# Half products joined, norm pairs, and one modulation group moved from TensorE to VectorE in a two-block float32 transformer kernel

## The chip, the cores and the metric

The program runs on one core of a Trainium2 chip. The metric is the device time of one execution in microseconds (us). The kernel before takes 2903.88 us (median of 3 runs, 2903.18 to 2905.7).

## What is computed

Four residual layers over 256 latent tokens and 256 context tokens of width 2048, float32 throughout. In every layer both streams are normalised and modulated, projected in, mixed, projected out and added back through a gate:

```python
shift, scale, gate = jnp.split(silu(c) @ mod_w[i] + mod_b[i], 3)      # one row for latent, one for context
h  = rms_norm(x,   norm_g[i]) * (1 + scale)  + shift
hc = rms_norm(ctx, norm_g[i]) * (1 + cscale) + cshift
y, yc = mixer(h @ w_in, hc @ w_in) @ w_out
x, ctx = x + gate * y, ctx + cgate * yc        # the context only where it is needed later
```

Layer 0 mixes with a gated linear recurrence (RG-LRU), layer 1 with differential attention over 16 heads. Layers 2 and 3 join a spatial gating unit (SGU, 8 groups) with grouped-query attention (8 heads); they have a context of their own (ctx_2) and condition vectors of their own. Layers 1 and 3 need no context output, so their out projections have 256 columns; those of layers 0 and 2 have 512.

## The kernel before

**Strips.** Every projection weight is cut into strips: 16 tiles of 128x128, 1 MB, one output tile of 128 rows each; there are 248. Strips stream through four half slots `raw` (two strips, `load_strip` on SyncE's queue). A float32 product is made from split halves: ScalarE rounds the weights to `w_hi` (`split_hi`, L221), VectorE takes the rest, `w_lo = raw - w_hi` (`split_lo`, L229), the activations lie as `h_hi` and `h_lo`, and TensorE runs three products per weight tile (`strip`, L247 to L249): high by high, high by low, low by high. `w_hi` and `w_lo` hold two strips, so the weights of strip s+2 are made while strip s+1 runs, and only after strip s is done. Each engine has its own written order of instructions (`lru_pe`, `lru_dve`, ...) and the engines meet in semaphores.

**Modulation.** The 4 x 3 x 2048 modulation values for two condition rows are products of a condition vector with 201 MB of weights, worked in beside the strips in two ways. A *group* (`mod_load`, `mod_chunk`, `mod_rows`, `mod_turn`, `mod_add`) gives 512 values: 4 chunks of 1 MB, 4 products each on TensorE (L261), a copy on ScalarE, a turn by small products (L284). A *unit* (`unit_load`, `unit`) gives 128 values on VectorE: two halves of 512 KB, and per half two multiply-and-accumulate passes over 1024 elements (L334 for the latent row, L336 for the context row), then one small add (L339). Units need the condition rows as silu(c) in `cb` (`cb_load` on GpSimd's queue, `cb_tanh` on ScalarE, `cb_silu` on VectorE, L304, L311, L318). `UNIT_PLAN` says how many whole units stand behind each tile of the out projections of layers 0 and 2. A half's slot is loaded again once VectorE has used it. Layer 3's scale is made by 4 groups (`SGU_MODS`, `M_SGU`) in layer 2's first four SGU groups; layer 3's shift by units in layer 2's out projection, its gate by units in layer 3's SGU.

**Out projection** (`out_first`, `out_pe`, `out_act`, `out_dve`, `out_pool`): 16 tiles in two PSUM banks. After tile m VectorE adds it to the residual (L651, L653) and splits strip m+2; in layers 0 and 2 its units follow. ScalarE splits, then squares the new tile (L557, L558), GpSimd adds the squares (L600) and scales x for the next norm (L602), and issues the units' loads (L326). In layer 1 the squares wait for the load of ctx_2.

**Norm** (`norm_pe`, `norm_sqrt`, `norm_act`, `norm_dve`): small products (L401) sum the squares, 1/sqrt comes back as rows (L406, L416), and then VectorE and ScalarE make h tile by tile (L453, L454, L436, L461). The first strip of the next layer takes each k tile of h as it becomes ready (`operand=` of `strip`); the second strip comes after it.

## Time and profile before

| | before |
|---|---|
| median of 3 runs | 2903.88 us |
| the profiled execution | 2906.17 us |
| its span, first to last instruction | 2904.5 us |
| TensorE (PE) busy | 2716.9 us, 94% |
| PE weight loads (PEld) busy | 2184.1 us, 75% |
| VectorE (DVE) busy | 1847.6 us, 64% |
| ScalarE (ACT) busy | 1213.4 us, 42% |
| GpSimd (POOL) busy | 314.1 us, 11% |
| mean granted TensorE clock | 0.969 of full |
| moved | 488.89 MB, 168 GB/s |

The profile is one execution; times in it are counted from its first instruction. Busy is the union of an engine's own instructions; matmuls are pipelined and overlap in the records, so the pace of TensorE is read from the distance of their starts, not from their durations. A bracket behind a row of the timeline is the idle time of that engine before the row and what ended it. The layers' stretches are: layer 0 with the start 0 to 745 us (its out projection from 570), layer 1 to 1615 (out projection from 1527), layer 2 to 2430 (SGU 1620 to 1950, out projection from 2257), layer 3 to the end.

### The profile page before, as it was taken

The page shows a single profiled execution, that of the slowest core. Times are in us where ns is not written, and L with a number is a line of the kernel's source. Part 1 is how long each engine was busy: PE and PEld are TensorE (multiplying, and loading weights), DVE is VectorE, ACT ScalarE, POOL GpSimd, SP SyncE. Part 2 cuts the span into 40 slices and gives each one's busy share as a digit, 9 for nine tenths or more (in the row PEclk, how much of TensorE's full clock was granted, in tenths as well). Part 3 has the DMA queues.
Part 4 walks back from the last instruction along what each step waited for, and adds up shares of the span by engine and source line. Part 5 has one row for each costly group of instructions (what it writes and reads, how often), then busy time and mean ns, then how long its engine had stood idle before and what let it go on. Part 6 is the DMA issues. An engine that isn't in the chain of part 4 may idle for free.

```text
span 2904.5 us, 41776 instructions
## 1 busy us (share of the span) xinstructions
PE 2716.9 (94%) x14482; PEld 2184.1 (75%) x14482; DVE 1847.6 (64%) x2772; ACT 1213.4 (42%) x1859; POOL 314.1 (11%) x437
## 2 busy tenths in 40 slices
PE   5799999889899999999989899999998998999989
PEld 1477777668677777777779677888886776998879
DVE  4399999889656565565665522334545887775654
ACT  3355655512434434443444422323444314553643
POOL 1111001044000000000004100000000442110000
PEclk7899999999999999999999999999999997999999
DMA  9755445367455554455535454322221664883325
GB/s 377 276 173 180 153 158 184 127 212 231 143 190 187 181 196 167 180 182 187 179 116 188 157 181 149 98 95 87 73 72 44 214 206 128 278 281 114 127 93 168
DMA packets 118631, 488.89 MB, mean 168 GB/s; under 512 B 13584, under 2 KB 15632, under 8 KB 103440
## 3 DMA queue, kind: packets, MB, share of 16 engines
q1 hardware_dynamic: 74176, 267.49, 27.3%
q0 software_dynamic: 44368, 220.22, 22.4%
q8 instruction: 56, 0.92, 0.1%
q14 instruction: 31, 0.25, 0.0%
HBM read 485.56 MB, written 2.10 MB: 168 GB/s over the span
## 4 chain that ended last, share of the span: by engine, by line
PE 67%; DVE 17%; issue 7%; DMA 5%; ACT 2%; DVEq 1%; POOL 0%; ACTq 0%; POOLq 0%; SPq 0%
PE psum L247 17%; PE psum L249 17%; PE psum L248 17%; DVE psum L334 4%; DVE w_lo L229 4%; PE psum L261 3%; DMA work<-in_mod_units 2%; DVE work L336 2%; DMA y<-in_mod_weights 2%; PE psum L974 1%; PE psum L1457 1%; PE psum L937 1%; DVE work L820 1%; ACT w_hi L221 1%; PE psum L284 1%
## 5 line engine op out<-in xcount | busy, mean ns | idle before, releaser
L247 PE MATMUL psum<-h_hi,w_hi 128*128 128x512 f32 (+1 forms) x3808 | 1359.8, 357 | 59.6 <-DVE h_lo L461 33.8
L249 PE MATMUL psum<-h_hi,w_lo 128*128 128x512 f32 (+1 forms) x3808 | 1323.6, 348 | 0.0
L248 PE MATMUL psum<-h_lo,w_hi 128*128 128x512 f32 (+1 forms) x3808 | 1323.0, 347 | 0.0
L229 DVE TENSOR_TENSOR w_lo<-raw,w_hi 128x1024 fp32r<-128x1024 f32 x496 | 597.5, 1246 | 587.9 <-ACT w_hi L221 587.8
L247 PEld LDWEIGHTS psum<-h_hi,w_hi 128*128 128x128 f32 x3808 | 728.6, 191 | 180.5 <-DVE w_lo L229 38.3
L248 PEld LDWEIGHTS psum<-h_lo,w_hi 128*128 128x128 f32 x3808 | 729.6, 192 | 93.7 <-issue 10.0
L249 PEld LDWEIGHTS psum<-h_hi,w_lo 128*128 128x128 f32 x3808 | 728.7, 191 | 88.7
L221 ACT ACTIVATE w_hi<-raw 128x1024 fp32r<-128x1024 f32 x496 | 496.7, 1052 | 283.0 <-PE psum L249 269.5
L334 DVE SCALAR_TENSOR_TENSOR psum<-work,modraw 128x1024 f32<-128x1024 f32 x128 | 177.7, 1389 | 24.3 <-DMA work<-in_mod_units 24.0
L336 DVE SCALAR_TENSOR_TENSOR work<-work,modraw 128x1024 f32<-128x1024 f32 x128 | 162.2, 1267 | 0.0
L267 POOL DMA_DIRECT2D modraw<-in_mod_weights x80 | 42.4, 530 | 822.6 <-PE psum L261 813.4
L261 PE MATMUL psum<-modraw,cond 128*32 128x512 f32 x768 | 110.8, 655 | 12.1 <-DMA modraw<-in_mod_weights 8.8
L326 POOL DMA_DIRECT2D work<-in_mod_units x128 | 68.1, 532 | 490.4 <-DVE work L336 473.1
L557 ACT ACTIVATE work<-xl 128x256 f32 (+1 forms) x48 | 19.8, 413 | 198.5 <-DVE xl L653 191.0
L600 POOL TENSOR_TENSOR work<-work 128x512 f32<-128x512 f32 x39 | 74.4, 1909 | 81.7 <-ACT work L558 81.7
L1001 ACT ACTIVATE y<-psum 128x512 f32<-128x512 f32 x16 | 9.6, 597 | 169.6 <-PE psum L249 169.6
L531 PE MATMUL psum<-h_hi,w_hi 128*128 128x256 f32 (+1 forms) x128 | 49.5, 386 | 30.0 <-DVE h_lo L516 30.0
L726 PE MATMUL psum<-work 128*128 128x512 f32 x128 | 59.2, 605 | 19.1 <-DVE work L820 19.1
L1027 ACT ACTIVATE y<-psum 128x512 f32<-128x512 f32 x16 | 9.6, 597 | 146.1 <-PE psum L249 146.1
L653 DVE SCALAR_TENSOR_TENSOR xl<-psum,mod,xl 128x256 f32 (+1 forms) x48 | 23.1, 481 | 67.3 <-PE psum L249 66.0
L1082 DVE RECIPROCAL work<-work 128x256 f32<-128x256 f32 x16 | 28.0, 1753 | 50.0 <-ACT work L1014 50.0
L726 PEld LDWEIGHTS psum<-work 128*128 128x128 f32 x128 | 23.0, 190 | 48.6 <-issue 40.2
(260 smaller groups left out, 2705.0 us busy)
## 6 DMA issues: line engine op xcount, KB each, us to landing
raw<-in_weights SPq DMA_DIRECT2D x496, 512.0 KB, 4.5
modraw<-in_mod_weights POOLq DMA_DIRECT2D x96, 1024.0 KB, 5.3
work<-in_mod_units POOLq DMA_DIRECT2D x128, 512.0 KB, 4.5
y<-in_mod_weights POOLq DMA_DIRECT2D x16, 1024.0 KB, 8.9
modraw<-in_mod_units POOLq DMA_DIRECT2D x32, 512.0 KB, 4.6
modraw<-in_cond_rows POOLq DMA_DIRECT2D x4, 1024.0 KB, 6.4
work<-in_gate_w POOLq DMA_DIRECT2D x16, 256.0 KB, 5.0
work<-in_x_t POOLq DMA_DIRECT2D x16, 256.0 KB, 3.6
```

The costliest lines, as they stand in the source:

```text
L221: act.activation(w_hi[:, par, half, :], raw[:, 2 * par + half, :], ACT.Copy).then_inc(S["split_hi"], 1)
L229: dve.tensor_tensor(w_lo[:, par, half, :], raw[:, 2 * par + half, :], w_hi[:, par, half, :].bitcast(F32), ALU.subtract).then_inc(S["split_ ...
L247: pe.matmul(dst, hi, h_hi[:, k, 0:n], start=(k == 0), stop=False)
L248: pe.matmul(dst, hi, h_lo[:, k, 0:n], start=False, stop=False)
L249: mm = pe.matmul(dst, lo, h_hi[:, k, 0:n], start=False, stop=(k == KT - 1))
L261: mm = pe.matmul(bank[32 * j:32 * j + 32, :], cond[:, 4 * q + j, :], chunk[:, j, :], start=(q == 0), stop=(q == 3))
L326: pool.dma_start(mw[:, half, :], ins["mod_units"][2 * p + half]).then_inc(unit_in[half], 16)
L334: dve.scalar_tensor_tensor(out=junk, in0=mw_work[:, half, :], scalar=0.5, in1=cb[:, 0, part], op0=ALU.mult, op1=ALU.mult, accum_out=macc[: ...
L336: dve.scalar_tensor_tensor(out=mw_work[:, half, :], in0=mw_work[:, half, :], scalar=0.5, in1=cb[:, 1, part], op0=ALU.mult, op1=ALU.mult, a ...
L531: pe.matmul(psum[:, c, 0:n], hi, h_hi[:, k, 0:n], start=(k == 0), stop=False)
L600: pool.tensor_tensor(acc, acc, sqb[c], ALU.add).then_inc(S["sq_added"], 1)
L726: pe.matmul(psum[:, GATE_BANK + g, :], lw["gw"][par][:, g, :], lw["xc"], start=True, stop=True).then_inc(L["gate_done"], 1)
```

## The change

1. **Layers 1 and 3, out projection.** `h_hi` and `h_lo` become two halves of one tensor `h_both`. `both` multiplies a high weight tile with 256 columns of h's high part and 256 of its low part in one product of 512 columns, which leaves two half results in a bank; the low weights add 256 columns. VectorE adds both half results to x, one after the other, with a semaphore between.
2. **Norm pair.** The first two strips of layers 1, 2 and 3 run together, k tile by k tile (`first_pair`), as layer 0's did. Two of the three sums of squares run in and behind the last strip of the out projection (`norm_sums`). The split of the second strip's second half stands behind the first four tiles of h.
3. **Layer 3's scale** comes from 16 units in layer 2's SGU, four halves per SGU group (`light`), loaded into the free upper half of y; the 4 TensorE groups are gone. The second network's condition rows are therefore prepared twice: in the first two tiles of layer 1's out projection, and in layer 2's as before.
4. **Halves.** The plan of layers 0's and 2's out projections counts half units behind each tile (`HALVES`), at most 3, and their tiles are written out instead of looped.

```diff
-        h_hi = sb("h_hi", [P, KT, NT], F32R)
-        h_lo = sb("h_lo", [P, KT, NT], F32R)
+        h_both = sb("h_both", [P, 2, KT, NT], F32R)
+        h_hi, h_lo = h_both[:, 0, :, :], h_both[:, 1, :, :]
...
+        def both(pe, bank, k, hi, lo):
+            joined = bank.rearrange("p (a t) -> p a t", a=2)
+            if k < KT - 1:
+                pe.matmul(joined, hi, h_both[:, :, k, 0:T], start=(k == 0), stop=False)
+                return pe.matmul(bank[:, 0:T], lo, h_hi[:, k, 0:T], start=False, stop=False)
+            pe.matmul(bank[:, 0:T], lo, h_hi[:, k, 0:T], start=False, stop=False)
+            return pe.matmul(joined, hi, h_both[:, :, k, 0:T], start=False, stop=True)
...
+        def first_pair(pe, s, dsts, ready, k0, k1):
+            for k in range(k0, k1):
+                half, kk = divmod(k, HALF)
+                pe.wait_ge(S["h_ready"], ready + k + 1)
+                for c, (dst, n) in enumerate(dsts):
+                    if kk == 0:
+                        pe.wait_ge(S["split_lo"], 2 * (s + c) + half + 1)
+                    hi, lo = (w[:, c, half, kk * P:(kk + 1) * P] for w in (w_hi, w_lo))
+                    pe.matmul(dst, hi, h_hi[:, k, 0:n], start=(k == 0), stop=False)
+                    pe.matmul(dst, hi, h_lo[:, k, 0:n], start=False, stop=False)
+                    mm = pe.matmul(dst, lo, h_hi[:, k, 0:n], start=False, stop=(k == KT - 1))
+                    if k == KT - 1:
+                        mm.then_inc(S["strip_done"], 1)
...
+        mw_y = y[:, 0, HALF:, :].rearrange("p (h k) t -> p h (k t)", h=2)
...
+        CB_NET = [0, 1, 1]
+        CB_IN = [1, 2 + 2 * (MOD_GROUPS - MOD_FIRST), 3 + 2 * (MOD_GROUPS - MOD_FIRST)]
...
+            if half == 1:
+                dve.wait_ge(S["unit_used"], 2 * p + 2)
+                dve.scalar_tensor_tensor(out=mod[:, bass.ds(slot, 1), :], in0=macc[:, par:par + 1, :, 0], scalar=col("mod_b", slot),
+                                         in1=macc[:, par:par + 1, :, 1], op0=ALU.add, op1=ALU.add).then_inc(S["unit_cols"], 1)
+                dve.wait_ge(S["unit_cols"], p + 1)
...
-        UNIT_PLAN = {0: [(0, 1, 2, 2), (1, 4, 1, 1), (4, 5, 2, 1), (5, 6, 1, 1), (6, 7, 1, 1), (7, 8, 0, 0)],
-                     1: [(0, 1, 0, 0), (1, 7, 0, 0), (7, 8, 0, 0)],
-                     2: [(0, 1, 0, 0), (1, 2, 2, 2), (2, 4, 1, 1), (4, 5, 2, 2), (5, 6, 1, 1), (6, 7, 1, 1), (7, 8, 0, 0)],
-                     3: [(0, 7, 0, 0), (7, 8, 0, 0)]}
...
+        HALVES = {0: (U_OUT0 - 1, [2, 1, 2, 2, 3, 2, 3, 2, 3, 3, 3, 2, 3, 3, 0, 0]),
+                  2: (U_OUT2, [0, 0, 2, 3, 3, 2, 3, 3, 2, 3, 3, 2, 3, 3, 0, 0])}
+        def halves_of(l, m):
+            if l not in HALVES:
+                return []
+            p, counts = HALVES[l]
+            n = sum(counts[:m])
+            return [(p + (n + i) // 2, (n + i) % 2) for i in range(counts[m])]
...
+        def norm_sums(pe, l, parts):
+            for n in parts:
+                sq = (acc, sqb[0], sqb[1])[n]
+                if n == 0:
+                    pe.wait_ge(S["sq_added"], added_base[l + 1])
+                    ge(pe, S["unit_used"], 2 * UNITS_READY[l])
+                else:
                     pe.wait_ge(S["sq_done"], KT * (l + 1) - 2 + n)
                 for t in range(NT // P):
                     mm = pe.matmul(psum[:, SS_BANK, t:t + 1], sq[:, t * P:(t + 1) * P], ones[:, 0:1],
                                    start=(n == 0 and t == 0), stop=(n == 2 and t == NT // P - 1))
-            mm.then_inc(S["ss_done"], 1)
+            if n == 2:
+                mm.then_inc(S["ss_done"], 1)
+        def norm_pe(pe, l):
+            norm_sums(pe, l, (2,) if l > 0 else (0, 1, 2))
...
+            high(0)
+            split_hi(act, layer_strip[l] // 2, 1, halves=(1,))
+            with act.Fori(1, KT // 4) as j:
+                high(j)
...
+            four(0)
+            split_lo(dve, layer_strip[l] // 2, 1, halves=(1,))
+            with dve.Fori(1, KT // 4 - 1) as j:
+                four(j)
...
+                    if wide[l]:
+                        pe.matmul(psum[:, c, 0:n], hi, h_hi[:, k, 0:n], start=(k == 0), stop=False)
+                        pe.matmul(psum[:, c, 0:n], hi, h_lo[:, k, 0:n], start=False, stop=False)
+                        mm = pe.matmul(psum[:, c, 0:n], lo, h_hi[:, k, 0:n], start=False, stop=(k == KT - 1))
+                    else:
+                        mm = both(pe, psum[:, c, :], k, hi, lo)
...
+            one(KT // 2 - 1, 0)
+            one(KT // 2 - 1, 1, (lambda half: norm_sums(pe, l + 1, ((0,), (1,))[half])) if l < 3 else None)
...
+                if l == 1:
+                    if c == 0:
+                        act.wait_ge(S["mod_cols"], MOD_GROUPS)
+                    cb_tanh(act, 1, (2 * c, 2 * c + 1))
...
+                        for p, half in halves_of(l, 2 * j + c):
+                            if p + 1 not in (U_SGU2, U_SGU):
+                                unit_load_half(pool, p + 1, half, mw_work)
...
+                else:
+                    dve.scalar_tensor_tensor(out=xl[:, m, :], in0=psum[:, c, T:NT], scalar=gate(0),
+                                             in1=xl[:, m, :], op0=ALU.mult, op1=ALU.add).then_inc(S["x_half"], 1)
+                    dve.wait_ge(S["x_half"], KT * (l // 2) + m + 1)
...
+                if isinstance(j, int) and j == 0 and l == 1:
+                    cb_silu(dve, 1, (2 * c, 2 * c + 1))
...
+            pool.wait_ge(S["mod_used"], 4 * MOD_GROUPS)
+            cb_load(pool, 1)
...
+                    first_pair(pe, S_ATT, [(psum[:, K_BANK, :], NT), (psum[:, Q_BANK, 0:T], T)], KT, 0, KT)
+                    for q in range(2):
+                        chunk(q)(1)
...
+            unit_load(pool, first, mw)
+            with pool.Fori(0, GROUPS // 2 - 1) as j:
+                for par in range(2):
+                    units(2 * j + par)
+                    table(2 * j + 2 + par, par, False)
+            units(GROUPS - 2)
+            unit_load(pool, first + KT - 1, mw)
...
+                    first_pair(pe, layer_strip[2 + lay], [(psum[:, GU_BANK, 0:n], n), (psum[:, GV_BANK, 0:n], n)], KT * (2 + lay), 0, KT)
...
-                    if mods:
-                        mod_chunk(pe, M_SGU + i, 3)
-                        mod_turn(pe, M_SGU + i, 1)
...
+                if lay == 0:
+                    unit_half(dve, U_SGU2 + 2 * i + n // 2, n % 2, n // 2, 9 * KT + SCALE + 2 * i + n // 2, mw_y)
```

Three places show how the order moves.

VectorE in layer 2's SGU, the second group from the split that follows its second strip on (`work` holds most buffers, `modraw` the condition rows, `y` in the change the unit's weights), before:

```order
L229 TENSOR_TENSOR w_lo<-raw,w_hi 128x1024 x2
L1303 SCALAR_TENSOR_TENSOR work<-work,psum 128x512
L229 TENSOR_TENSOR w_lo<-raw,w_hi 128x1024 x2
L1308 TENSOR_REDUCE small<-work 128x4
L291 TENSOR_TENSOR mod<-psum,cols 128x8
L1312 RECIPROCAL small<-small 128x4
L1316 TENSOR_SCALAR work<-psum,small 128x128 x4
```

With the change:

```order
L228 TENSOR_TENSOR w_lo<-raw,w_hi 128x1024 x2
L376 SCALAR_TENSOR_TENSOR psum,small<-y,modraw 128x1024
L378 SCALAR_TENSOR_TENSOR y,small<-y,modraw 128x1024
L382 SCALAR_TENSOR_TENSOR mod<-small,cols 128x2
L1360 SCALAR_TENSOR_TENSOR work<-work,psum 128x512
L228 TENSOR_TENSOR w_lo<-raw,w_hi 128x1024 x2
L376 SCALAR_TENSOR_TENSOR psum,small<-y,modraw 128x1024
L378 SCALAR_TENSOR_TENSOR y,small<-y,modraw 128x1024
L1365 TENSOR_REDUCE small<-work 128x4
L1367 RECIPROCAL small<-small 128x4
L1371 TENSOR_SCALAR work<-psum,small 128x128 x4
L376 SCALAR_TENSOR_TENSOR psum,small<-y,modraw 128x1024
```

A half unit (L376 and L378, every second one with the add L382) now stands behind each split and another behind the scaled tiles; the add for the TensorE group, L291, is gone.

ScalarE at the start of layer 1's out projection, from the last high copy of y on, before:

```order
L511 ACTIVATE h_hi<-y 128x256
L221 ACTIVATE w_hi<-raw 128x1024 x2
L557 ACTIVATE work<-xl 128x256
L558 ACTIVATE work<-y 128x256
L221 ACTIVATE w_hi<-raw 128x1024 x2
L557 ACTIVATE work<-xl 128x256
L558 ACTIVATE work<-y 128x256
```

With the change:

```order
L572 ACTIVATE h_both<-y 128x256
L220 ACTIVATE w_hi<-raw 128x1024 x2
L629 ACTIVATE work<-xl 128x256
L630 ACTIVATE work<-y 128x256
L350 ACT_TABLE_LOAD
L350 ACTIVATE work<-modraw 128x1024 x2
L220 ACTIVATE w_hi<-raw 128x1024 x2
L629 ACTIVATE work<-xl 128x256
L630 ACTIVATE work<-y 128x256
L350 ACTIVATE work<-modraw 128x1024 x2
```

The tanh of the condition rows stands between the first tile's squares and the next strip's split, with a table load ahead of it.

TensorE at the start of layer 2, before, where the next rows go on with the first strip alone:

```order
L401 MATMUL psum<-consts,work 128x1 x12
L406 MATMUL psum<-consts,small 128x128 x4
L247 MATMUL psum<-h_hi,w_hi 128x512
L248 MATMUL psum<-h_lo,w_hi 128x512
L249 MATMUL psum<-h_hi,w_lo 128x512
L247 MATMUL psum<-h_hi,w_hi 128x512
L248 MATMUL psum<-h_lo,w_hi 128x512
L249 MATMUL psum<-h_hi,w_lo 128x512
```

With the change (each weight tile pair of the first strip is followed by the second strip's, to the end of both):

```order
L451 MATMUL psum<-consts,work 128x1 x8
L460 MATMUL psum<-consts,small 128x128 x4
L285 MATMUL psum<-h_both,w_hi 128x512
L286 MATMUL psum<-h_both,w_hi 128x512
L287 MATMUL psum<-h_both,w_lo 128x512
L285 MATMUL psum<-h_both,w_hi 128x512
L286 MATMUL psum<-h_both,w_hi 128x512
L287 MATMUL psum<-h_both,w_lo 128x512
L285 MATMUL psum<-h_both,w_hi 128x512
L286 MATMUL psum<-h_both,w_hi 128x512
```

The two strips' products alternate by k tile, and four of the twelve sums of squares (L401, now L451) have left this place for the middle of the last strip; the next four stand directly behind that strip.

## Rows read from the trace of the kernel before

**Rows 1.** The page, part 4: the chain that ended last, by engine.

```profile
PE 67%; DVE 17%; issue 7%; DMA 5%; ACT 2%; DVEq 1%; POOL 0%; ACTq 0%; POOLq 0%; SPq 0%
```

**Rows 2.** Waits of TensorE: us in total, times, longest.

```profile
PE psum L247 <- DVE h_lo L461: 33.8, 42, 4.5
```

**Rows 3.** Timeline of TensorE (start us, us), two 512-column and two 256-column products.

```profile
742.75 0.39 PE L247 MATMUL psum<-h_hi,w_hi 128*128 128x512 f32 x1
742.98 0.39 PE L248 MATMUL psum<-h_lo,w_hi 128*128 128x512 f32 x1
...
1560.01 0.28 PE L249 MATMUL psum<-h_hi,w_lo 128*128 128x256 f32 x1
1560.13 0.28 PE L247 MATMUL psum<-h_hi,w_hi 128*128 128x256 f32 x1
```

**Rows 4.** Timeline of VectorE, layer 2's SGU: groups 1 and 2, then 4 and 5.

```profile
1715.83 0.69 DVE L1303 SCALAR_TENSOR_TENSOR work<-work,psum 128x512 f32<-128x512 f32 x1 [8.80 <-ACT work L1253]
...
1756.56 0.69 DVE L1303 SCALAR_TENSOR_TENSOR work<-work,psum 128x512 f32<-128x512 f32 x1 [8.80 <-ACT work L1253]
...
1835.63 0.69 DVE L1303 SCALAR_TENSOR_TENSOR work<-work,psum 128x512 f32<-128x512 f32 x1 [7.57 <-ACT work L1253]
...
1869.68 0.69 DVE L1303 SCALAR_TENSOR_TENSOR work<-work,psum 128x512 f32<-128x512 f32 x1 [7.49 <-ACT work L1253]
...
1893.83 2.36 DVE L229 TENSOR_TENSOR w_lo<-raw,w_hi 128x1024 fp32r<-128x1024 f32 x2 [5.78 <-ACT w_hi L221]
```

**Rows 5.** Timeline of ScalarE and VectorE, first strips of layers 2 and 3.

```profile
1650.24 0.60 ACT L1243 ACTIVATE work<-psum 128x512 f32<-128x512 f32 x1 [0.67 <-PE psum L249]
1662.35 0.60 ACT L1248 ACTIVATE work<-psum 128x512 f32<-128x512 f32 x1 [9.63 <-PE psum L249]
...
2462.47 0.39 ACT L1243 ACTIVATE work<-psum 128x256 f32<-128x256 f32 x1 [0.71 <-PE psum L249]
2463.84 2.36 DVE L229 TENSOR_TENSOR w_lo<-raw,w_hi 128x1024 fp32r<-128x1024 f32 x2 [2.46 <-ACT w_hi L221]
2470.12 0.39 ACT L1248 ACTIVATE work<-psum 128x256 f32<-128x256 f32 x1 [5.38 <-PE psum L249]
```

**Rows 6.** Windows: us, busy us (instructions) by engine, granted clock, DMA share, GB/s.

```profile
2432.50:2466.60 34.10, 21.93 (x77) 17.28 (x77) 29.42 (x69) 19.96 (x39) 2.17 (x4) 0.50 0.22 62
```

**Rows 7.** TensorE's groups by line, out projections of layers 0 and 2.

```profile
L247 PE MATMUL psum<-h_hi,w_hi 128*128 128x512 f32 x224 | 89.1, 398 | 12.3 <-DVE w_lo L229 12.3
...
L247 PE MATMUL psum<-h_hi,w_hi 128*128 128x512 f32 x222 | 88.7, 399 | 9.6 <-DVE w_lo L229 9.6
```

**Rows 8.** Timeline of VectorE and GpSimd, layer 0's out projection: units.

```profile
584.87 1.23 DVE L334 SCALAR_TENSOR_TENSOR psum<-work,modraw 128x1024 f32<-128x1024 f32 x1 [5.83 <-DMA work<-in_mod_units]
587.16 1.23 DVE L334 SCALAR_TENSOR_TENSOR psum<-work,modraw 128x1024 f32<-128x1024 f32 x1
...
597.06 0.53 POOL L326 DMA_DIRECT2D work<-in_mod_units  x1 [1.99 <-DVE work L336]
...
601.75 1.23 DVE L334 SCALAR_TENSOR_TENSOR psum<-work,modraw 128x1024 f32<-128x1024 f32 x1 [2.44 <-DMA work<-in_mod_units]
...
696.34 0.48 DVE L651 SCALAR_TENSOR_TENSOR y<-psum,mod,work 128x256 f32<-128x256 f32 x1
...
705.88 0.48 DVE L651 SCALAR_TENSOR_TENSOR y<-psum,mod,work 128x256 f32<-128x256 f32 x1
```

**Rows 9.** Timeline, layer 1's out projection, and ScalarE's tanh (ns min/median/max).

```profile
1536.99 0.42 ACT L557 ACTIVATE work<-xl 128x256 f32<-128x256 f32 x1 [7.46 <-DMA y<-in_ctx_t]
...
1540.17 0.39 PE L247 MATMUL psum<-h_hi,w_hi 128*128 128x256 f32 x1 [3.37 <-DVE w_lo L229]
...
L311 ACT ACTIVATE work<-modraw x8: 1041/1054/1062, 131.1 to 2268.6; 128x1024 f32<-128x1024 f32 x8
L311 ACT ACT_TABLE_LOAD  x1: 1283/1283/1283, 129.4 to 129.4; - x1
```

**Rows 10.** Timeline of TensorE, sums of squares before layer 1.

```profile
743.43 2.94 PE L401 MATMUL psum<-consts,work 128*128 128x1 f32 x24
```

272 lines of the change are left out of this document (115 added, 157 removed).

## The prediction

> **What bounds the kernel now.** I read first the chain that ended last: 67% of it is TensorE, 17% VectorE [rows 1]. The second view is TensorE's own waits, because an idle microsecond there is worth a microsecond: the longest sum, 33.8 us, is its wait for h, in the norms [rows 2], and in the out projections of layers 0 and 2 it waits 12.3 and 9.6 us for low weights [rows 7]. The third is TensorE's pace where it waits for nothing: 227 ns from one 512-column product to the next, 120 ns at 256 columns [rows 3], so a strip is 48 x 0.227 = 10.9 us or 48 x 0.120 = 5.76 us. The kernel is bound by TensorE's issue nearly everywhere; what counts is work taken off TensorE, and waits of TensorE that go or come.
>
> **Layer 3's scale leaves TensorE.** In layer 2's SGU a group with modulation takes 1756.56 - 1715.83 = 40.73 us, one without 1869.68 - 1835.63 = 34.05 us [rows 4]: 6.7 us a group, 4 groups, -26.7 us; I take -26.5. In return VectorE gets 32 half units. A half is 587.16 - 584.87 = 2.3 us [rows 8], with the small add 9.7 us per group of 34. They are free if they fit where VectorE idles: in the groups without modulation it waits 5.8 us before a split [rows 4], and 7.5 us before L1303. A half of 2.3 us fits ahead of each. The loads come four to a 34 us group, far apart against the 601.75 - 597.06 = 4.7 us from issue to landing [rows 8]; GpSimd's queue holds only tables between them. Without that cover a half costs its 2.3 us.
>
> **Norm pair.** VectorE's and ScalarE's pace of h is untouched, so the last k tile is ready as late as before; what goes is the second strip behind it. But no weights of a third strip can be made before both of the pair are done, and that is a new wait. In layer 3 the first strip's result is read at 2462.47 and VectorE begins the next split at 2463.84; half a split later (1.2 us), 2.6 us after the read began and 3.0 after the strip, TensorE can go on [rows 5]. Layer 2: second strip now 10.9 us behind the first; then one more k tile (3 x 0.227 = 0.7) and the 3.0 wait: -7.2 us. Layer 3: now 2470.12 - 2462.47 = 7.65 us [rows 5], as TensorE ran at half its clock (1.2 GHz) until 2466.6 after a norm in which it had little to do [rows 6]; then 0.4 + 3.0: -4.3. Layer 1: the second strip has 256 columns, 5.8 us; two modulation chunks stand behind the pair and cover 2 of the 3.5 us: -5. Sum 16.5; I take -16, since the pair is denser work for a slowed clock but the new wait may bring another slow stretch. Nothing is late next: the following strips find their splits early. Bounds: -20 (no new wait) and -9 (the wait and a slow stretch behind each).
>
> **Sums of squares.** 24 small products take 2.9 us, 0.11 each, mostly while ScalarE squares the last tile [rows 10]. Eight of them go into the last strip, where they are on the path: 0.9 us, three times, less what the end gains; VectorE is late there in two of the three. +1.2 us (0 to 2.7).
>
> **Joined halves.** Per weight tile three 256-column products, 3 x 0.120 = 0.360, become 0.227 + 0.120 = 0.347 [rows 3]: 13 ns, over 2 x 16 x 16 tiles 6.7 us. The rows give 13 ns of fixed time per product over N/2.4. By the Trainium skill (TensorE: Matmul & The Clock Gate, Back-to-back issue gap) the isolated distance of two matmuls is N/2.4 + 2.5 ns, which speaks against this edit: one product less would be worth 2.5 ns, 1.3 us in all. The trace decides for 13 ns. VectorE's second add, 0.48 us as L651's [rows 8], hides behind ScalarE's split, except after each layer's last tile: +0.9. Net -5.8 (0 if one 512-column product costs as much as two of 256).
>
> **Condition rows in layer 1.** ScalarE squares the first tile at 1536.99, when ctx_2 has landed, and TensorE's fourth strip waits until 1540.17 [rows 9]. Now a table load (1.28) and two tanh (2 x 1.05) stand between those squares and the fourth strip's split: squares done 1537.7, tanh 1541.1, first half high 1542.1. VectorE, after two silu passes of about 1.2 and two adds, splits from 1543.7: TensorE starts at 1544.9, +4.7. The second pair of tanh and silu does the same with less: +1.2. After 8 us of idling some half clock follows: +2. Sum +7.9 (3 to 11). The second load of the condition rows, 2 MB, goes out behind the last group's weights long before ctx_2's, and costs nothing.
>
> **Halves.** In layer 0 a tile with a whole unit takes 705.88 - 696.34 = 9.54 us on VectorE [rows 8], of a strip of 10.9: 4.6 us for the tile (with what GpSimd's adds hold up) and 2.3 a half, 0.24 for the add. Double units overran, behind tiles 0, 1 and 8. The new plan spreads the same halves; its tiles with 3 still have one wait: the third half's load is issued when the first is used, lands 4.7 later, and the second half covers 2.4, so 2.3 us of waiting and 14.1 us a tile. I walked both plans tile by tile: tile m starts on VectorE at the later of strip m's end and its own end of tile m-1; low weights for strip m+2 are there 4.2 us after; TensorE starts strip m+2 at the later of that and the end of strip m+1. The old plan so walked stands 10.4 us in layer 0 and 8.5 in layer 2 (traced: 12.3 and 9.6 [rows 7]), the new one 6.8 and 9.4, mostly in tiles 11 to 15, where 3, 3 and 3 follow each other. With the slow stretches after the old stalls, and one tile evacuated late: -6 in layer 0, -1.3 in layer 2. With landings in 4.0 us it stalls 2.9 and 4.8; with 5.5, 11.9 and 15.3.
>
> **Sum.** -26.5 - 16 + 1.2 - 5.8 + 7.9 - 6 - 1.3 = -46.5 us. The profiled execution took 2906.2, so 2859.7; the median run lies 2.3 lower, 2857.4. Forecast **2857 us**.
>
> **Rivals.**
> - *Third halves land late.* The out projections load 1.5 MB of units beside 1 MB of weights per tile. For: VectorE already waited 2.4 and 5.8 us there [rows 8]. Against: those loads ran beside the same weights. At 5.5 us landing 5 + 6 us more stalls, and 2 of half clock: 2870. Chance 0.20.
> - *Landings are quick and the new waits short.* At 4.0 us the walk loses 8.5 us of stalls, with 4 of half clock: 2845. Chance 0.17.
> - *The join does nothing*: the change does not do what it says if the two half streams are walked apart and a 512-column product costs 240 ns. 2864. Against: every 512-column product takes 227 ns. Chance 0.05.
> - *Slower: half units ahead of the splits in layer 2's SGU.* VectorE's order is fixed, so a half that comes late holds the split behind it, and TensorE a strip later. If each of the 32 held TensorE for its full 2.3 us and the adds 4: +78, 2857 + 78 = 2935. It decides once VectorE's idle time ahead of a split is under 2.3 us; the rows have 5.8. Chance 0.02.
>
> **The numbers.** Main case 0.56 (2850 to 2865). The range takes in the first two rivals and the bounds of pair and condition rows: 2843 to 2874; about 1 in 10 lies outside on each side at most. A measurement can tell about 0.2%, 6 us: faster 0.97, within it 0.01, slower 0.02.
>
> **What would show it.** Layer 2's SGU: all groups at 34 us, no wait of TensorE for low weights. Norms: no idle time per k tile worth a second strip, but one wait of about 3 us behind each pair in layers 2 and 3, 1 to 2 in layer 1. Layer 1's out projection: a wait of 8 us ahead of the fourth strip, then starts of weight tiles 0.347 apart. Layers 0 and 2: VectorE waiting some 2.3 us for a load in each tile with three halves, TensorE for low weights near the end. It is wrong if a 34 us group grows, if the pair's end moves against h's last tile, or if the stalls in layers 0 and 2 go altogether.

## The result and the profile after

The changed kernel takes 2875.94 us in the median of four runs (2873.26 to 2877.19), the kernel before, beside it, 2904.3: a ratio of 0.9902, 95% interval 0.9888 to 0.9916. That is 28.4 us gained, where 46.5 were forecast, and 2 us above the upper end of the range.

| | after |
|---|---|
| the profiled execution | 2876.43 us |
| its span | 2874.7 us |
| TensorE (PE) busy | 2694.6 us, 94% |
| VectorE (DVE) busy | 1942.7 us, 68% |
| mean granted TensorE clock | 0.967 of full |

The page of after, part 4, the chain that ended last: TensorE holds 65% of it, 2 points less than in [rows 1], and VectorE 20%, 3 points more.

```profile
PE 65%; DVE 20%; issue 7%; DMA 6%; ACT 2%; DVEq 1%; POOL 0%; ACTq 0%; POOLq 0%; SPq 0%
```

The waits of TensorE over the whole span (us in total, times, longest), beside [rows 2] and [rows 7]:

```profile
PE psum L285 <- DVE h_both L518: 16.6, 23, 3.7
PE psum L246 <- DVE w_lo L228: 15.6, 7, 3.2
PE psum L451 <- DVE work L378: 10.9, 2, 6.1
PE psum L259 <- DVE w_lo L228: 8.6, 3, 8.0
```

L285 is `first_pair`, L246 `strip`, L259 the joined product, L451 the sums of squares. The wait for h fell from 33.8 us to 16.6, as the pair should make it. The third row is new: 10.9 us, in two waits, in which TensorE stands ahead of the sums of squares until VectorE's last half unit is through.

**Where the time went.** I cut both spans at the same places, by the end of a strip's last product in TensorE's timeline, and do so for every kernel run below (one profiled execution each, us). "Out+norm" is an out projection with the norm behind it, up to the end of the fourth strip of the next layer. A column called a stage below is one of these:

| | up to layer 0's out | layer 0 out+norm | attention | layer 1 out | norm, layer 2 up to its out | layer 2 out+norm | layer 3 up to its out | layer 3 out |
|---|---|---|---|---|---|---|---|---|
| before | 537.9 | 266.4 | 690.1 | 122.3 | 588.9 | 276.2 | 301.2 | 118.4 |
| after | 536.8 | 264.4 | 690.2 | 125.8 | 555.9 | 278.7 | 302.8 | 116.5 |
| sums_behind | 535.8 | 264.2 | 691.8 | 126.4 | 555.4 | 278.4 | 304.1 | 116.8 |
| sums_own_bank | 533.2 | 262.0 | 690.2 | 126.7 | 555.6 | 275.3 | 304.0 | 115.1 |
| before_sums_moved | 533.6 | 265.6 | 690.1 | 122.6 | 592.1 | 282.5 | 301.2 | 116.8 |
| out_halves_short | 538.9 | 243.6 | 691.8 | 125.6 | 556.7 | 260.4 | 301.4 | 114.9 |
| whole_units | 535.3 | 252.8 | 690.2 | 126.1 | 555.5 | 265.9 | 303.8 | 115.0 |
| before_units_spread | 533.2 | 260.4 | 691.8 | 120.2 | 587.9 | 272.2 | 301.0 | 118.4 |
| pair_apart | 540.4 | 271.7 | 691.8 | 125.8 | 563.0 | 281.2 | 304.1 | 116.6 |
| join_apart | 537.8 | 266.2 | 691.7 | 127.7 | 555.3 | 278.0 | 301.0 | 116.8 |
| join_adjacent | 539.4 | 264.0 | 690.1 | 125.3 | 556.7 | 279.1 | 302.5 | 116.7 |
| rows_spread | 535.2 | 265.4 | 690.1 | 122.3 | 556.8 | 280.7 | 301.0 | 116.6 |
| sgu_halves_short | 539.1 | 267.0 | 690.1 | 125.6 | 555.6 | 278.3 | 301.0 | 115.1 |
| best | 539.9 | 254.3 | 690.2 | 121.8 | 555.3 | 269.9 | 305.8 | 116.8 |

Two things are scatter from one execution to the next. The first column moves by 7 us between kernels whose code is the same there. And stretches at half clock (a granted clock of 0.50, 1.2 GHz) come and go elsewhere: one of 3.4 us makes the 1.6 us more of after in the column of layer 3 up to its out; in layer 2's attention after has 13.6 us of them and before 6.8, and the 3.5 us more that it takes stand in the column of layer 2's out+norm. Differences of 3 us and less in one column mean little.

Read so, the change did in its stages: layer 0's out projection with its norm -2.0 (forecast -10.6: halves -6, pair -5, sums +0.4), layer 2's +2.5 (forecast -5.2), the norm and SGU of layer 2 -33.0 (forecast -33.3), layer 1's out projection +3.5 (forecast +5.0). The two stages that hold half units are short of the forecast by 16 us, 3.5 of them the scatter in layer 2's attention, and nothing else is off by more than 2.

Each of the two stages has two parts, the out projection up to the end of its last strip and the norm behind it. The norms are 4.7 and 4.9 us shorter than before (56.0 against 60.8, 48.0 against 52.9). Layer 0's out projection is 2.7 us longer (208.35 against 205.66), layer 2's 4.0 longer from the end of its second strip on (171.7 against 167.7). So it is the out projections that miss the forecast.

In layer 2's SGU every group takes what a group without modulation took, 1837.08 - 1803.02 = 34.06 us, early ones too (1734.88 - 1700.90 = 33.98), where [rows 4] had 40.73 for an early one. Timeline of VectorE, after (start us, us, ..., idle before it and who ended that):

```profile
1700.90 0.69 DVE L1360 SCALAR_TENSOR_TENSOR work<-work,psum 128x512 f32<-128x512 f32 x1 [5.10 <-ACT work L1311]
...
1734.88 0.69 DVE L1360 SCALAR_TENSOR_TENSOR work<-work,psum 128x512 f32<-128x512 f32 x1 [4.79 <-ACT work L1311]
...
1803.02 0.69 DVE L1360 SCALAR_TENSOR_TENSOR work<-work,psum 128x512 f32<-128x512 f32 x1 [4.80 <-ACT work L1311]
...
1837.08 0.69 DVE L1360 SCALAR_TENSOR_TENSOR work<-work,psum 128x512 f32<-128x512 f32 x1 [4.70 <-ACT work L1311]
```

The end of layer 0's out projection, timeline of VectorE, after. A third half (L376) waits for its load, 2.48 us in tile 12, 2.13 in tile 13; tile 13's is through at 735.5 us, tile 14 is taken (L727) at 735.79 only, 14 us after its strip ended (721.7). In the kernel before it was taken 1.8 us after (734.5 and 732.7):

```profile
719.06 1.24 DVE L376 SCALAR_TENSOR_TENSOR psum<-work,modraw 128x1024 f32<-128x1024 f32 x1 [2.48 <-DMA work<-in_mod_units]
...
721.36 0.48 DVE L727 SCALAR_TENSOR_TENSOR y<-psum,mod,work 128x256 f32<-128x256 f32 x1
...
733.12 1.23 DVE L376 SCALAR_TENSOR_TENSOR psum<-work,modraw 128x1024 f32<-128x1024 f32 x1 [2.13 <-DMA work<-in_mod_units]
734.27 1.22 DVE L378 SCALAR_TENSOR_TENSOR work<-work,modraw 128x1024 f32<-128x1024 f32 x1
...
735.79 0.48 DVE L727 SCALAR_TENSOR_TENSOR y<-psum,mod,work 128x256 f32<-128x256 f32 x1
...
738.40 2.36 DVE L228 TENSOR_TENSOR w_lo<-raw,w_hi 128x1024 fp32r<-128x1024 f32 x2 [1.74 <-ACT w_hi L220]
745.18 0.48 DVE L727 SCALAR_TENSOR_TENSOR y<-psum,mod,work 128x256 f32<-128x256 f32 x1 [4.42 <-PE psum L248]
```

And TensorE there: in the middle of the last strip the sums of squares wait 4.82 us, and behind the wait the products come 0.43 us apart (737.91, 738.34), where they come 0.227 apart at full clock:

```profile
730.44 0.39 PE L248 MATMUL psum<-h_both,w_lo 128*128 128x512 f32 x1
735.64 1.84 PE L451 MATMUL psum<-consts,work 128*128 128x1 f32 x8 [4.82 <-DVE work L378]
737.91 0.63 PE L247 MATMUL psum<-h_both,w_hi 128*128 128x512 f32 x1
738.34 0.63 PE L248 MATMUL psum<-h_both,w_lo 128*128 128x512 f32 x1
```

The granted clock (the column behind the five engines' busy times) is at its lower level, 1.2 GHz, for 6.8 us there and for 10.2 us at the like wait in layer 2's last strip, which ends at 2394.0. The first 0.6 and 3.6 us of them still lie in the waits. Behind them TensorE loses 3.0 and 3.2 us, by the starts of its products (those up to the first at full pace took 6.62 and 7.52 us, and would take 3.6 and 4.3 at the distances seen at full clock, 0.227 and for the sums 0.112):

```profile
735.00:741.80 6.80, 6.16 (x19) 5.22 (x20) 3.96 (x7) 2.62 (x4) 0.61 (x1) 0.50 0.12 41
2390.40:2400.60 10.20, 6.55 (x20) 5.52 (x21) 5.84 (x9) 2.62 (x4) 0.61 (x1) 0.50 0.13 48
```

### The profile page after: what moved, and what is told of

It is laid out like the page before. It is cut to its first block, busy times and chain, and to the rows that moved or that the text cites. A ratio compares the mean times of both kernels' runs of the same rounds, so it can differ in the third digit from the quotient of the medians.

```text
span 2874.7 us, 40435 instructions
## 1 busy us (share of the span) xinstructions
PE 2694.6 (94%) x13810; PEld 2159.6 (75%) x13810; DVE 1942.7 (68%) x2948; ACT 1217.1 (42%) x1861; POOL 314.5 (11%) x455
## 4 chain that ended last, share of the span: by engine, by line
PE 65%; DVE 20%; issue 7%; DMA 6%; ACT 2%; DVEq 1%; POOL 0%; ACTq 0%; POOLq 0%; SPq 0%
PE psum L246 15%; PE psum L248 15%; PE psum L247 15%; DVE w_lo L228 5%; DVE psum L376 4%; PE psum L259 4%; PE psum L296 3%; DVE work L378 2%; DMA work<-in_mod_units 2%; DMA y<-in_mod_weights 2%; PE psum L260 2%; PE psum L1509 1%; PE psum L1012 1%; PE psum L1050 1%; DVE work L890 1%
## 5 line engine op out<-in xcount | busy, mean ns | idle before, releaser
L246 PE MATMUL psum<-h_both,w_hi 128*128 128x512 f32 (+1 forms) x3264 | 1188.3, 364 | 15.7 <-DVE w_lo L228 15.6
L248 PE MATMUL psum<-h_both,w_lo 128*128 128x512 f32 (+1 forms) x3264 | 1158.6, 355 | 0.0
L247 PE MATMUL psum<-h_both,w_hi 128*128 128x512 f32 (+1 forms) x3264 | 1158.3, 355 | 0.0
L228 DVE TENSOR_TENSOR w_lo<-raw,w_hi 128x1024 fp32r<-128x1024 f32 x496 | 607.2, 1265 | 480.2 <-ACT w_hi L220 479.3
L246 PEld LDWEIGHTS psum<-h_both,w_hi 128*128 128x128 f32 x3264 | 620.9, 190 | 112.9 <-issue 15.4
L247 PEld LDWEIGHTS psum<-h_both,w_hi 128*128 128x128 f32 x3264 | 621.1, 190 | 93.5 <-issue 9.8
L248 PEld LDWEIGHTS psum<-h_both,w_lo 128*128 128x128 f32 x3264 | 620.3, 190 | 87.0
L376 DVE SCALAR_TENSOR_TENSOR psum<-work,modraw 128x1024 f32<-128x1024 f32 x128 | 171.3, 1338 | 36.5 <-DMA work<-in_mod_units 36.0
L259 PE MATMUL psum<-h_both,w_hi 128*128 128x512 f32 x480 | 177.7, 410 | 15.6 <-DVE w_lo L228 8.6
L378 DVE SCALAR_TENSOR_TENSOR work<-work,modraw 128x1024 f32<-128x1024 f32 x128 | 158.6, 1239 | 0.0
L260 PE MATMUL psum<-h_both,w_lo 128*128 128x256 f32 x480 | 137.2, 286 | 0.0
L259 PEld LDWEIGHTS psum<-h_both,w_hi 128*128 128x128 f32 x480 | 92.9, 194 | 39.9 <-DVE w_lo L228 9.5
L296 PE MATMUL psum<-modraw,cond 128*32 128x512 f32 x640 | 93.8, 669 | 10.5 <-DMA modraw<-in_mod_weights 6.9
L260 PEld LDWEIGHTS psum<-h_both,w_lo 128*128 128x128 f32 x480 | 93.4, 195 | 1.4
L1077 ACT ACTIVATE y<-psum 128x512 f32<-128x512 f32 x16 | 9.6, 597 | 169.7 <-PE psum L248 167.7
L285 PE MATMUL psum<-h_both,w_hi 128*128 128x512 f32 (+1 forms) x128 | 54.4, 425 | 20.3 <-DVE h_both L518 16.6
L676 POOL TENSOR_TENSOR work<-work 128x512 f32<-128x512 f32 x39 | 64.4, 1651 | 75.9 <-ACT work L630 75.9
```

The costliest lines, as they stand in the source:

```text
L228: dve.tensor_tensor(w_lo[:, par, half, :], raw[:, 2 * par + half, :], w_hi[:, par, half, :].bitcast(F32), ALU.subtract).then_inc(S["split_ ...
L246: pe.matmul(dst, hi, h_hi[:, k, 0:n], start=(k == 0), stop=False)
L247: pe.matmul(dst, hi, h_lo[:, k, 0:n], start=False, stop=False)
L248: mm = pe.matmul(dst, lo, h_hi[:, k, 0:n], start=False, stop=(k == KT - 1))
L259: pe.matmul(joined, hi, h_both[:, :, k, 0:T], start=(k == 0), stop=False)
L260: return pe.matmul(bank[:, 0:T], lo, h_hi[:, k, 0:T], start=False, stop=False)
```

## The experiments

Each was timed against the kernel before on its chip, and ratios stand with their 95% intervals. A time is the median of the kernel's runs. A row of the table above is one execution only.

### Is it the new place of the sums of squares?

**sums_behind.** The first suspicion: the half units' product and the sums of squares share a PSUM bank (`junk` is banks 6 and 7, `SS_BANK` is 6), so `norm_sums` waits for all half units of the layer, and it now does so in the middle of a strip. The run puts the sums of layers 0 and 2 back behind the strip.

```
-  one(KT // 2 - 1, 1, (lambda half: norm_sums(pe, l + 1, ((0,), (1,))[half])) if l < 3 else None)
+  one(KT // 2 - 1, 1, (lambda half: norm_sums(pe, l + 1, ((0,), (1,))[half])) if l == 1 else None)
...
-  norm_sums(pe, l, (2,) if l > 0 else (0, 1, 2))
+  norm_sums(pe, l, (2,) if l == 2 else (0, 1, 2))
```

> The changed kernel with the sums of squares of layers 0 and 2 back behind the last strip. Theory A: in the last strip they wait for VectorE's last half unit, because its product goes to the same PSUM bank; that wait (4.8 and 6.1 us in the trace of the changed kernel) and the half clock behind it (8.5 us) go away: 2857 us, no wait of TensorE ahead of L451 in the middle of the last strips. Rival B: the last half units are late for the norm in any case, which waits for them itself; the wait moves behind the strip: 2872 to 2876 us.

Measured: 2875.42 us, ratio 0.9899 (0.9884 to 0.9914): no change, rival B. Layer 0's out projection is now 7.4 us shorter (200.98 against 208.35) and the norm behind it 7.2 longer (63.2 against 56.0); in layer 2 it is 10.0 and 9.6. The waits of TensorE in layer 0's stage, and VectorE at its end, in sums_behind:

```profile
PE psum L246 <- DVE w_lo L228: 9.5, 5, 3.5
PE psum L451 <- ACT work L630: 4.0, 2, 3.2
PE psum L451 <- DVE work L378: 1.3, 1, 1.3
```

```profile
735.58 1.23 DVE L376 SCALAR_TENSOR_TENSOR psum<-work,modraw 128x1024 f32<-128x1024 f32 x1 [2.49 <-DMA work<-in_mod_units]
...
738.25 0.48 DVE L727 SCALAR_TENSOR_TENSOR y<-psum,mod,work 128x256 f32<-128x256 f32 x1
...
740.86 2.36 DVE L228 TENSOR_TENSOR w_lo<-raw,w_hi 128x1024 fp32r<-128x1024 f32 x2 [1.74 <-ACT w_hi L220]
743.14 0.48 DVE L727 SCALAR_TENSOR_TENSOR y<-psum,mod,work 128x256 f32<-128x256 f32 x1
```

VectorE is done with tile 13's third half at 738.0 us, then come tile 14 and its split, and tile 15, whose strip has long ended (736.8), is taken at 743.14. Its squares (ACT L630) are what the sums then wait for. Theory A was wrong: the new place of the sums only showed where VectorE was late.

**sums_own_bank.** The sums stay in the strip, in bank 5, and the wait for the half units moves behind them. (Bank 5 is in use at the kernel's start, so the sums of the very first norm are not the kernel's.)

```
-  ge(pe, S["unit_used"], 2 * UNITS_READY[l])
...
-  mm = pe.matmul(psum[:, SS_BANK, t:t + 1], sq[:, t * P:(t + 1) * P], ones[:, 0:1],
+  mm = pe.matmul(psum[:, SUM_BANK, t:t + 1], sq[:, t * P:(t + 1) * P], ones[:, 0:1],
...
   pe.wait_ge(S["rcol_done"], l + 1)
+  ge(pe, S["unit_used"], 2 * UNITS_READY[l])
```

> The changed kernel with the sums of squares in PSUM bank 5, which nothing else uses there, in their place within the last strip, and without the wait for the half units ahead of them (it now stands ahead of the broadcast products into bank 6). Theory A (the shared bank makes the wait): 2856 us, 1 us below the version with the sums behind the strip. Rival B (the place within the strip costs by itself, since the sums also need GpSimd's last add): still a wait in the middle of the strip, 2872 us or more.

Measured: 2878.77 us (2867.45 to 2882.85), ratio 0.9911 (0.9895 to 0.9928). No gain either by the medians; its profiled execution, the fastest of the five, is 2.4 and 3.4 us shorter in the two stages, which is about what the table can tell. The expectation had not thought of what stands here: no wait in the middle of the strip, but 1.31 and 3.83 us behind it, for tile 14's and tile 15's squares.

**before_sums_moved.** The kernel before with `norm_sums` in and behind the last strip and nothing else.

```
-  pe.wait_ge(S["x_new"], KT * l + 2 * j + c - 1)
-  strip(pe, st, psum[:, c, 0:n], n)
...
+  one(KT // 2 - 1, 0)
+  one(KT // 2 - 1, 1, (lambda half: norm_sums(pe, l + 1, ((0,), (1,))[half])) if l < 3 else None)
```

> The kernel before with nothing but the sums of squares moved into and behind the last strip. Theory A: its last whole unit is done at 734.2 us, 4 us ahead of the middle of the last strip, and 2419.2 us, 4 us ahead too; so the wait for it costs nothing, and it is the new plan of halves that makes the wait: 2901 to 2904 us, no wait ahead of the sums. Rival B (the place costs by itself): 2913 to 2924 us.

Measured: 2908.48 us, ratio 1.0013 (1.0004 to 1.0022), 1 to 6 us slower. No wait ahead of the sums is in its trace; the last strips of layers 0 and 2 are 0.9 us longer each (11.8 against 10.9), and nothing comes back that the scatter would let one see (norms of 61.2 and 52.7 us against 60.8 and 52.9). So the move by itself costs what the prediction said (+1.2, 0 to 2.7) or somewhat more, and the wait comes with the plan of halves.

### Is it the plan of halves?

**out_halves_short.** Half units of one column in the out projections of layers 0 and 2. The kernel so leaves out the modulation values that they make; their loads, waits and places stay.

```
-  part = slice(half * 1024, (half + 1) * 1024)
-  dve.scalar_tensor_tensor(out=junk, in0=mw[:, half, :], scalar=0.5, in1=cb[:, 0, part], op0=ALU.mult,
+  part = slice(half * 1024, half * 1024 + n)
+  dve.scalar_tensor_tensor(out=junk[:, 0:n], in0=mw[:, half, 0:n], scalar=0.5, in1=cb[:, 0, part], op0=ALU.mult,
...
```

> The changed kernel with the half units of the out projections of layers 0 and 2 reduced to one column each (their modulation columns are left out; loads, waits and order stay). Theory C (VectorE's time in these stages is what counts): all waits of TensorE for low weights and ahead of the sums go, 18 and 19 us: 2839 us. Rival B (the loads bound it): VectorE then waits for each load, two halves a strip still fit 10.9 us, but a third waits 4.7 us: some of the waits ahead of the sums stay, 2850 to 2870 us.

Measured: 2838.52 us, ratio 0.9778 (0.9758 to 0.9797), theory C's figure. VectorE now waits 46.9 us for the loads in layer 0's stage, and TensorE waits for none of it: L246's wait for low weights is absent from its waits there, whose longest two are these.

```profile
PE psum L285 <- DVE h_both L518: 7.3, 12, 3.7
PE psum L451 <- ACT work L630: 0.9, 1, 0.9
```

```profile
L376 DVE SCALAR_TENSOR_TENSOR psum<-work,modraw 128x1 f32<-128x1 f32 x34 | 15.0, 440 | 47.5 <-DMA work<-in_mod_units 46.9
```

So the loads alone hold nobody; with the passes of the 34 halves on top of its tiles VectorE holds TensorE. That is 37 us for the 66 halves of the two stages.

**whole_units.** The same halves in another order, with the sums behind the strip. The kernel to compare it with is sums_behind, which differs in the order alone.

```
-  HALVES = {0: (U_OUT0 - 1, [2, 1, 2, 2, 3, 2, 3, 2, 3, 3, 3, 2, 3, 3, 0, 0]),
-            2: (U_OUT2, [0, 0, 2, 3, 3, 2, 3, 3, 2, 3, 3, 2, 3, 3, 0, 0])}
+  HALVES = {0: (U_OUT0 - 1, [2, 2, 2, 2, 2, 4, 2, 2, 2, 2, 4, 2, 2, 2, 2, 0]),
+            2: (U_OUT2, [0, 0, 4, 2, 2, 2, 4, 2, 2, 2, 2, 4, 2, 2, 2, 0])}
...
```

> The changed kernel with the sums of squares of layers 0 and 2 behind the last strip and the halves dealt out evenly: layer 0 [2,2,2,2,2,4,2,2,2,2,4,2,2,2,2,0], layer 2 [0,0,4,2,2,2,4,2,2,2,2,4,2,2,2,0]. Theory C: VectorE's queue bounds these two stages; the new plan pays a wait for a load (2.2 to 2.6 us) in each of its nine tiles with three halves, and what VectorE is behind at the last tile with halves the norm waits for. A tile with 2 halves waits for nothing, one with 4 waits once. Walked with the measured durations, layer 0's last strip ends at 727 us, not at 745, and VectorE is done with the last tile at 729, not 746; layer 2's 2385 and 2388, not 2404 and 2405. 2844 us, no wait of TensorE for low weights in the two stages. Rival B (what was behind is bound to the loads themselves, 512 KB each beside the weights): 2865 to 2876 us.

Measured: 2848.95 us (2847.39 to 2849.92), ratio 0.9814 (0.9796 to 0.9831): 27 us below the changed kernel and 26.5 below sums_behind, most of what taking the halves away brings. It is 5 us above the 2844 that I expected, and low weights are still waited for, 3.6 and 2.4 us in the two stages, where I expected no such wait. The walk said that layer 0's last strip ends at 727 us: it ended at 727.7, though that owes something to luck, since the stage began 1.5 us earlier than in after; counted from the stage's start it is 2.2 us late. Layer 2's was to end 212 us behind the last strip of its attention, and ended 209.4 behind it. (The expectation counts nine tiles with three halves; the change's plan has seven in layer 0 and eight in layer 2.) Waits of TensorE in layer 0's stage, in whole_units:

```profile
PE psum L246 <- DVE w_lo L228: 3.6, 3, 1.8
PE psum L451 <- DVE work L378: 3.3, 1, 3.3
```

VectorE's waits for the loads (L376, L334 before), layer 0's stage, in after, then in sums_behind, in whole_units and in the kernel before:

```profile
L376 DVE SCALAR_TENSOR_TENSOR psum<-work,modraw 128x1024 f32<-128x1024 f32 x34 | 46.7, 1374 | 20.1 <-DMA work<-in_mod_units 19.9
```

```profile
L376 DVE SCALAR_TENSOR_TENSOR psum<-work,modraw 128x1024 f32<-128x1024 f32 x34 | 46.7, 1375 | 23.7 <-DMA work<-in_mod_units 23.5
```

```profile
L376 DVE SCALAR_TENSOR_TENSOR psum<-work,modraw 128x1024 f32<-128x1024 f32 x34 | 46.2, 1360 | 12.2 <-DMA work<-in_mod_units 12.2
```

```profile
L334 DVE SCALAR_TENSOR_TENSOR psum<-work,modraw 128x1024 f32<-128x1024 f32 x34 | 51.1, 1504 | 11.0 <-DMA work<-in_mod_units 11.0
```

Against sums_behind VectorE waits 11.3 us less for loads in layer 0's stage (12.2 against 23.5) and 10.9 less in layer 2's (5.9 against 16.8), and the stages are 11.4 and 12.5 us shorter. So the loads that VectorE waits for account for nearly all of what the new order gained: each third half waited 1.4 to 2.6 us for its load, seven and eight times in after; a tile with four halves waits once, as one with three does, and there are two and three of those. Against the kernel before, the change's plan added 9 us of waiting in layer 0's stage (19.9 against 11.0), and 6.3 in layer 2's (15.0 against 8.7).

**before_units_spread.** The kernel before with its whole units, dealt out in the same places.

```
-  UNIT_PLAN = {0: [(0, 1, 2, 2), (1, 4, 1, 1), (4, 5, 2, 1), (5, 6, 1, 1), (6, 7, 1, 1), (7, 8, 0, 0)],
+  UNIT_PLAN = {0: [(0, 1, 1, 1), (1, 2, 1, 1), (2, 3, 1, 2), (3, 5, 1, 1), (5, 6, 2, 1), (6, 7, 1, 1), (7, 8, 1, 0)],
...
```

> The kernel before with its whole units dealt out as in whole_units (layer 0: one a tile, two at tiles 5 and 10, none at 15; layer 2: one a tile from tile 3 on, two at tiles 2, 6 and 11), nothing else. Theory C (VectorE's time and its waits for loads bound the two stages, halves are not needed): no wait of TensorE for low weights, 15 us less in each of the two, less 4 us each that the norm waits for the last tile: 2882 us. Rival (the halves themselves bring what whole_units gained): 2895 to 2904 us.

Measured: 2893.37 us (2889.44 to 2900.99), ratio 0.9964 (0.9951 to 0.9978): a gain of 11 us, half of what I expected. In the two stages the spread is worth 6.0 and 4.0 us by the table. The out projections themselves gain 11.8 and 11.1 us, but 5.8 and 7.1 of them are lost in the norm behind, not 4, since tile 14 now carries a unit: TensorE waits for it ahead of the sums,

```profile
PE psum L247 <- DVE w_lo L229: 3.4, 2, 2.3
PE psum L401 <- DVE work L336: 3.3, 1, 3.3
```

and then for tile 15. Halves are hardly needed for that gain: with the pair's 5.0 and 4.9 us in the norms (pair_apart, below) this kernel would stand at about 255.4 and 267.3 in the two stages, an estimate, and whole_units stands at 252.8 and 265.9.

### The other parts

**pair_apart.** Strip by strip in place of `first_pair` in layers 1, 2 and 3.

```
-  first_pair(pe, S_ATT, [(psum[:, K_BANK, :], NT), (psum[:, Q_BANK, 0:T], T)], KT, 0, KT)
...
+  strip(pe, att_strip(j, par, 0), psum[:, K_BANK, :], NT, chunk(0), operand=(S["h_ready"], KT))
+  strip(pe, att_strip(j, par, 1), psum[:, Q_BANK, 0:T], T, chunk(1))
...
```

> The changed kernel with the first two strips of layers 1, 2 and 3 one after the other again. Theory: the pair is worth 3.8, 7.1 and 3.7 us by the two traces, once the sums of squares and the modulation chunk are taken off: 2890.5 us. Rival: the gain at the norms is that of the moved sums and of the split that now stands behind four tiles of h, and the new wait for weights behind the pair eats the pair's own: 2876 to 2879 us.

Measured: 2895.53 us (2890.16 to 2900.05), ratio 0.9964 (0.9951 to 0.9977): the pair is worth 19.6 us by the medians, 16.9 by the table (7.3, 7.1 and 2.5). Of the 7.3 and 2.5, which lie in the stages of the out projections, +2.4 and -2.4 fall in the out projections themselves, where the two kernels are the same; the norms alone give 5.0 (61.0 against 56.0) in front of layer 1 and 4.9 (52.9 against 48.0) in front of layer 3. In after the wait behind the pair is 2.2 us in layer 2 and 2.4 in layer 3 (L246's, of the 15.6 above). Timeline of ScalarE in after: both results are read 2.4 us apart, where [rows 5] had 12.1:

```profile
1652.04 0.60 ACT L1301 ACTIVATE work<-psum 128x512 f32<-128x512 f32 x1 [0.78 <-PE psum L287]
...
1654.42 0.59 ACT L1306 ACTIVATE work<-psum 128x512 f32<-128x512 f32 x1
```

**join_apart.** Three 256-column products and one add again.

```
-  pe.matmul(joined, hi, h_both[:, :, k, 0:T], start=(k == 0), stop=False)
+  pe.matmul(bank[:, 0:T], hi, h_hi[:, k, 0:T], start=(k == 0), stop=False)
+  pe.matmul(bank[:, 0:T], hi, h_lo[:, k, 0:T], start=False, stop=False)
...
```

> The changed kernel with three products of 256 columns per weight tile again in layers 1's and 3's out projections, and one add. By the starts in its trace (0.353 us a weight tile against 0.360) the join is worth 3.4 us, less 0.9 for the second add behind each last tile: 2878.4 us. By the prediction's 13 ns: 2881.8 us. If the join does nothing: 2875 us.

Measured: 2883.29 us (2879.23 to 2887.51), ratio 0.9929 (0.9916 to 0.9943). By the medians the join is worth 7 us, but the starts below say 3.4 less 0.9, and the out projections of layers 1 and 3 are 1.9 and 0.3 us longer in join_apart (127.7 against 125.8, 116.8 against 116.5). The rest is within what the first column does from run to run. Timeline of TensorE in after, layer 3's out projection:

```profile
2839.86 0.40 PE L259 MATMUL psum<-h_both,w_hi 128*128 128x512 f32 x1
2840.10 0.28 PE L260 MATMUL psum<-h_both,w_lo 128*128 128x256 f32 x1
2840.22 0.40 PE L259 MATMUL psum<-h_both,w_hi 128*128 128x512 f32 x1
2840.46 0.28 PE L260 MATMUL psum<-h_both,w_lo 128*128 128x256 f32 x1
2840.57 0.40 PE L259 MATMUL psum<-h_both,w_hi 128*128 128x512 f32 x1
```

The joined product takes 236 ns to the next, the 256-column one behind it 117: 353 a weight tile, not 347.

**join_adjacent.** Low parts right behind the high ones in SBUF, `h_hi[:, k, :]` as the joined operand.

```
-  pe.matmul(joined, hi, h_both[:, :, k, 0:T], start=(k == 0), stop=False)
+  pe.matmul(joined, hi, h_hi[:, k, :], start=(k == 0), stop=False)
...
-  dve.tensor_tensor(h_view(h_lo, l, k), y_view(l, k), h_view(h_hi, l, k).bitcast(F32),
+  dve.tensor_tensor(h_view(h_lo, l, k) if wide[l] else h_hi[:, k, T:NT], y_view(l, k), h_view(h_hi, l, k).bitcast(F32),
...
```

> The changed kernel with the low parts of h in layers 1's and 3's out projections put right behind the high parts, so that the joined product reads 512 columns in one piece. In the trace of the changed kernel the joined product takes 236 ns to the next one, 9 ns more than any other product of 512 columns. Theory: the 9 ns are the jump between two pieces; they go, 512 x 9 ns = 4.6 us: 2871.3 us, weight tiles 0.347 apart. Rival: they come from the change of width between products or from the bank's second half: 2875.9 us, weight tiles 0.353 apart.

Measured: 2879.47 us (2877.05 to 2884.67), ratio 0.9922 (0.9905 to 0.9939). The distance stays 236 ns, so two pieces are not its cause. Where two weight tiles' order is turned (L261, L262), a 256-column product ahead of another still takes 0.12 and the joined one ahead of another joined one 0.24:

```profile
2845.13 0.28 PE L260 MATMUL psum<-h_both,w_lo 128*128 128x256 f32 x1
2845.25 0.28 PE L261 MATMUL psum<-h_both,w_lo 128*128 128x256 f32 x1
2845.37 0.40 PE L262 MATMUL psum<-h_both,w_hi 128*128 128x512 f32 x1
2845.61 0.40 PE L259 MATMUL psum<-h_both,w_hi 128*128 128x512 f32 x1
2845.84 0.28 PE L260 MATMUL psum<-h_both,w_lo 128*128 128x256 f32 x1
```

So the change of width does not explain it either, and neither does the bank's second half: the wide strips' products of 512 columns fill a whole bank too and come 227 ns apart. What the 9 ns are stays open.

**rows_spread.** The condition rows' tanh and silu, one at a time behind tiles 2 to 5.

```
+  for m in range(2, 6):
+      tile(m // 2, m % 2, False)
+      cb_tanh(act, 1, (m - 2,))
...
```

> The changed kernel with the condition rows' tanh and silu in layer 1 taken one at a time behind tiles 2 to 5, not two each behind tiles 0 and 1. Theory: the wait ahead of the fourth strip goes back from 7.96 to 3.4 us, and at tiles 2 to 5 ScalarE (3 us of a strip of 5.6) and VectorE (3.4 us) have room for 1.05 and 1.2 us: 2871.5 us. Rival: with the table load and the tanh between, ScalarE or VectorE falls behind the short strips and the time comes back there: 2876 us.

Measured: 2873.29 us (2870.56 to 2874.06), ratio 0.9896 (0.9878 to 0.9914). The wait ahead of the fourth strip falls from 7.96 to 4.22 us, and the column by 3.5 (after first, then rows_spread):

```profile
1540.73 0.79 PE L259 MATMUL psum<-h_both,w_hi 128*128 128x512 f32 x1 [7.96 <-DVE w_lo L228]
```

```profile
1536.85 0.50 PE L259 MATMUL psum<-h_both,w_hi 128*128 128x512 f32 x1 [4.22 <-DVE w_lo L228]
```

**sgu_halves_short.** Layer 2's 32 halves in the SGU at one column each, by the edit of out_halves_short in `light`. The kernel so leaves out layer 3's scale.

> The changed kernel with the 32 half units in layer 2's SGU reduced to one column each (layer 3's scale is left out; loads and order stay). Theory: they lie in idle time of VectorE and cost nothing: 2876 us. Rival: each holds TensorE a little; every 0.3 us of it is 10 us: 2866 us or less.

Measured: 2881.97 us (2877.26 to 2885.85), ratio 0.9924 (0.991 to 0.9937). Norm and SGU of layer 2 take 555.6 us, in after 555.9: the halves are free there. That the median is 6 us higher with less work says how far medians of five runs are to be trusted.

**best.** The edits of whole_units and rows_spread together.

> whole_units and rows_spread together: 2849 us, less the 3.7 us that the wait ahead of the fourth strip fell in rows_spread, is 2845 us. If the two share a saving, 2849 us.

Measured: 2850.83 us (2843.43 to 2859.24), ratio 0.9804 (0.9791 to 0.9818). Layer 1's out projection has the 4 us of rows_spread (121.8 against 126.1), the whole has not: its runs scatter over 16 us, and its profiled one, the slowest of the five, is 4.6 us longer than whole_units' in the first column and 4.0 in layer 2's out and norm, where the two kernels are the same. No better than whole_units, so far as this measures; both beat the changed kernel by 25 to 27 us.

## Why the prediction was wrong

**Layer 3's scale, -26.5: right.** Groups of 34.0 us, no wait in them, and halves that cost nothing. With layer 2's pair the column gained 33.0, forecast 33.3.

**Norm pair, -16: right**, measured 17 to 20. The waits behind it were 2.2 and 2.4 us, not 3.0. The three norms gave 5.0, 7.1 and 4.9 us where 5, 7.2 and 4.3 were put down. For layer 1 that is partly luck: the terms named there, 5.8 us less the 1.5 of the wait that is not covered, make 4.3, not 5.

**Sums of squares, +1.2: right by itself**, or a little low (1 to 6 us in before_sums_moved). What it left out, the two waits of 10.9 us in all with half clock behind them, costs nothing beyond what the next point costs: without them, in sums_behind, the time is the same.

**Halves, -6 and -1.3: wrong, and this is the step that failed.** With the sums' share, -5.6 and -0.9 were forecast for the out projections of layers 0 and 2. In after layer 0's is 2.7 us longer than before and layer 2's, from its second strip on, 4.0; in pair_apart, which has the halves and the sums but not the pair, 5.1 and 3.8. That is a miss of 8 to 11 us and of 5, so 13 to 15 of the 18.5 us between forecast and result. (The plan of halves was not run alone on the kernel before. The sums' share rests on before_sums_moved, and 3.5 us of the rest are scatter in layer 2's attention.)

The walk through the tiles was right as far as it went. It gave 6.8 and 9.4 us of waits for low weights; the trace has 5.7 and 5.2. But it asked only when TensorE can start each strip, and ended with the last start. By its own 14.1 us for a tile with three halves, against strips of 10.9, VectorE falls behind, and I read that delay off only where a strip wanted weights. Behind tile 13 no strip does; tile 14's and tile 15's results do, their squares, the norm. Carried on to VectorE's own end with the prediction's durations, the walk has VectorE take tile 15 at about 168 us of the out projection in layer 0 with either plan, and in layer 2 at about 171 with the new plan and 166 with the old (an estimate): no gain in one layer and a loss in the other.

The traces show the same. In the kernel before VectorE had been done with tile 13 at 734.2 us of a last strip ending at 743.6; in after at 735.5, though the strips up to tile 14's had ended 11 us earlier. The 12.3 us of stalls in the middle of the stage fell to 5.7, and VectorE's lateness was paid at the end in their place. By sums_behind it does not matter whether TensorE pays in the last strip or behind it. By out_halves_short the loss goes when VectorE's passes go, and by whole_units when the waits for third halves go, which the prediction had at their right price, 2.3 us each, but let cost nothing at the end. Walked again with VectorE's own end in view, the same durations gave the length of whole_units' two out projections to 2.2 and 2.6 us before it ran.

**Joined halves, -5.8: half.** 7 ns a weight tile, not 13: 3.4 us less 0.9. The trace's rule (fixed 13 ns a product) did not hold for the mixed widths. By the Trainium skill (TensorE: Matmul & The Clock Gate, Back-to-back issue gap), with 2.5 ns a product on top of N/2.4, it would have been 1.3 us, an estimate. The trace does not agree: its 7 ns lie between, and its 236 and 117 ns follow neither rule.

**Condition rows, +7.9: too high.** The wait ahead of the fourth strip was 7.96 us, as the walk said (8), so the first term, +4.7, was right (7.96 - 3.37 = 4.6), but neither the second pair of tanh (+1.2) nor more half clock (+2) showed: about +4.6 in all. By rows_spread 3.5 to 3.7 us of it can be had back.

The rivals named a cause near it (third halves landing late, 2870), but the third halves waited 1.4 to 2.6 us where I had put down 2.3; the waits were about as assumed, only their consequence was not.

## What to carry to other kernels

A plan for an engine's queue of work is judged by when that queue ends, not by the stalls that are seen now: removing stalls in the middle can merely move them to the end. Where a load is issued when its buffer is freed and two buffers alternate, a third piece in one place costs a wait of its own (here about 2.3 us), and a fourth costs no second wait, so extra pieces are best dealt out in pairs, with work behind them that can wait. Where a kernel makes a product wait for another engine's last write to the same PSUM bank, moving the product forward moves that wait forward with it; look at what stands behind the wait before removing it.

## What the runs showed of the hardware

A joined product of 512 columns ahead of one of 256, or of another joined one, took 236 ns from start to start where every product of 512 among its like took 227. The 256-column one ahead of a joined one took 117 against 120 among its like. Both held with the operand in one piece and in two.

TensorE's clock fell at waits. From 540 us on after has thirteen waits of TensorE of 3.0 us or more, and a stretch at 1.2 GHz began in or just behind each of them, for instance 6.8 us at the wait of 4.8 and 10.2 us at the one of 6.1. Products of 512 columns then stood 0.43 us apart in place of 0.23, from 737.9 to 741.8 us in after. In these two places TensorE lost 3.0 and 3.2 us on top of the waits. At the seven waits between 2.0 and 3.0 us such a stretch stood four times, and in sums_behind two waits of 3.4 and 3.2 us (ending at 2322.1 and 2359.4) had none, so the length of a wait alone does not tell.

A load of half a unit, 512 KB, that is issued when its buffer is freed took 4.4 us to land in the median of after (4.7 in [rows 8]). Beside the other buffer's half a third half so cost VectorE a wait of 1.4 to 2.6 us, in all fifteen tiles that had one.
